# An encoder kernel on Trainium2: the first output weights split inside attention, the first output unit multiplied there

## The reference

```python
h = rms_norm(x, norm_mix_pre[l])
z = h @ w_in[l]                        # split into heads of three kinds
oa = mla_mixer(...)                    # 4 heads, latent attention, rotary key
ob = dilated_mixer(...)                # 4 heads, dilated windows and a relative bias
oc = gqa_axial_mixer(...)              # 8 query heads on 2 key heads
mix = concatenate([oa, ob, oc]) @ w_out[l]
x = x + rms_norm(mix, norm_mix_post[l])
h = rms_norm(x, norm_ffn_pre[l])
x = x + rms_norm(conv_gated_mlp(h, w_up[l], conv_w[l], conv_b[l], w_down[l]), norm_ffn_post[l])
```

## Time and profile before

| what | value |
|---|---|
| median of 3 runs | 3733.16 us (3732.81 to 3735.91) |
| the profiled execution's own time | 3736.56 us |
| its span in the profile | 3734.7 us |
| mean granted clock of TensorE | 0.988 |
| PE, DVE, ACT, POOL busy | 97%, 49%, 42%, 30% |
| attention of layer 0, layer 1 (barrier to barrier) | 324.7 to 806.3, 2169.4 to 2649.9 us |
| projection of layer 0, layer 1 | 806.3 to 965.6, 2649.9 to 2809.4 us |

### The profile page before, as it was taken

The page is one execution under the profiler, slowest core; times in us unless marked ns, Lnnn a source line. Parts: engine busy times, 40 slices in busy tenths (PEclk is TensorE's granted clock), DMA queues, the critical chain, the costliest instruction groups (busy, mean ns, idle before and its releaser), DMA issues. The chain is left out here.

```text
span 3734.7 us, 49829 instructions
## 1 busy us (share of the span) xinstructions
PE 3638.0 (97%) x18267; PEld 3008.3 (81%) x18267; DVE 1846.1 (49%) x2900; ACT 1564.6 (42%) x2527; POOL 1138.5 (30%) x827
## 2 busy tenths in 40 slices
PE   8999999989999999999999999999899999999998
PEld 7787777768788888888767877777788888888886
DVE  4135868954543333444551367699363333344335
ACT  4344878974311222221342367789552221221213
POOL 1233443433412221221342334433343221221213
PEclk9999999999999999999999999999999999999999
DMA  5442321023111111111324323110231111111113
GB/s 172 126 108 67 77 66 33 22 69 102 46 34 45 39 34 39 34 45 34 113 67 142 97 71 81 47 40 26 68 102 46 40 37 36 39 39 34 34 45 113
DMA packets 205964, 233.99 MB, mean 63 GB/s; under 512 B 15968, under 2 KB 164486, under 8 KB 205767
## 3 DMA queue, kind: packets, MB, share of 16 engines
q1 hardware_dynamic: 205807, 231.93, 21.1%
HBM read 173.86 MB, written 51.48 MB: 60 GB/s over the span
## 5 line engine op out<-in xcount | busy, mean ns | idle before, releaser
L222 PE MATMUL ps<-hh,wh 128*128 128x512 f32 (+1 forms) x2688 | 969.9, 361 | 15.4 <-PEq L216 11.5
L223 PE MATMUL ps<-hl,wh 128*128 128x512 f32 (+1 forms) x2688 | 955.9, 356 | 0.0
L224 PE MATMUL ps<-hh,wl 128*128 128x512 f32 (+1 forms) x2688 | 954.9, 355 | 0.0
L2466 POOL TENSOR_TENSOR wl<-raw,wh 128x1024 fp32r<-128x1024 f32 x126 | 301.7, 2401 | 1267.2 <-ACT wh L2299 1267.2
L222 PEld LDWEIGHTS ps<-hh,wh 128*128 128x128 f32 x2688 | 510.7, 190 | 93.8 <-issue 18.0
L2527 DVE SCALAR_TENSOR_TENSOR cb<-ps,params,cb 128x1023 f32<-128x1023 f32 (+1 forms) x172 | 143.9, 878 | 870.4 <-ACT cb L2308 870.4
L223 PEld LDWEIGHTS ps<-hl,wh 128*128 128x128 f32 x2688 | 511.0, 190 | 76.3 <-issue 5.7
L224 PEld LDWEIGHTS ps<-hh,wl 128*128 128x128 f32 x2688 | 510.1, 190 | 72.1
L1557 DVE TENSOR_TENSOR pl<-ps,ph 128x512 fp32r<-128x512 f32 (+1 forms) x576 | 375.0, 652 | 54.3 <-ACT ps L1402 53.9
L1511 DVE TENSOR_REDUCE mx<-ps 128x1 f32<-128x512 f32 x480 | 330.5, 689 | 141.8 <-PE ps L1316 82.9
L1401 ACT ACTIVATE ph<-ps 128x512 fp32r<-128x512 f32 (+1 forms) x576 | 329.6, 572 | 157.5 <-PE ps L1282 152.3
(11 more groups left out here) (265 smaller groups left out, 5644.8 us busy)
## 6 DMA issues: line engine op xcount, KB each, us to landing
raw<-in_w_up SPq DMA_DIRECT2D x88, 512.0 KB, 3.9
heads<-stage SPq DMA_DIRECT2D x38, 640.0 KB, 3.1
raw<-in_w_down SPq DMA_DIRECT2D x44, 512.0 KB, 3.7
rq<-heads SPq DMA_DIRECT2D x56, 320.0 KB, 4.8
raw<-in_w_in SPq DMA_DIRECT2D x32, 512.0 KB, 4.4
rk<-heads SPq DMA_DIRECT2D x32, 320.0 KB, 4.7
raw<-in_w_out SPq DMA_DIRECT2D x16, 512.0 KB, 4.3
residual<-my SPq DMA_DIRECT2D x32, 256.0 KB, 2.0
```

What stands on the lines that cost most here:

```text
L222: pe.matmul(out, wh, xh, start=(k == 0), stop=False)
L223: pe.matmul(out, wh, xl, start=False, stop=False)
L224: last = pe.matmul(out, wl, xh, start=False, stop=(k == len(pairs) - 1))
L2466: pool.tensor_tensor(c.wl[slot][:], c.raw[parity][:], c.wh[slot][:].bitcast(F32), ALU.subtract).then_inc(w_lo, units)
```

## The change

- **Attention.** SP now loads six units of w_out: 0 and 1 as before, 2 to 5 each when the unit two before it has its low part. It waits at the end for all six. GpSimd splits units 0 to 3 itself, high part by a copy and low part by a subtraction (`split_out_weights`), at steps 5 and 11 of heads 14 and 15, ahead of the output splits of these steps. After its last matmul of attention PE waits for the last two side results (bank 1 is theirs), the low part of unit 0 and the split output block 0 of head 15, and multiplies output unit 0 of block 0 into bank 1. A semaphore `early_unit` tells the next phase.
- **Projection.** PE starts with unit 1; whoever waited for `unit_done` waits for `early_unit` (unit 0) or one less. ScalarE starts with the evacuation of unit 0, splits units 4, 5, then 6 and 7; GpSimd makes the low parts of units 4 to 7. SP loads units 6 and 7. `early_unit` joins the list of semaphores cleared at the end of this phase.
- **Tiles.** Twelve weight tiles lie behind `my` and are dealt out so that the ones written in attention lie over memory that the last heads don't use; units 6 and 7 of w_out use wh0, wl0, wh1, wl1; units 0 and 1 of w_up the tiles of output units 0 and 1, unit 2 of w_up wh2, wl2.
- **Tables.** The table loads at the head of ScalarE's streams in attention and in projection are gone.

```diff
--- before.py
+++ after.py
@@ -164,6 +164,7 @@
     c.q2 = [take("q2_0", [P, T], F32R), q2_1, take("q2_2", [P, T], F32R)]
+    k1_0_at = at[0]
     c.k1 = [take("k1_0", [P, T], F32R), k1_1]
@@ -180,9 +181,10 @@
     c.my = [take(f"my{i}", [P, KC, 512]) for i in range(2)]
-    c.mw_hi, c.mw_lo = list(c.wh[0:2]), list(c.wl[0:2])
-    c.mw_hi += [take(f"mw_hi{n}", [P, KC, P], F32R) for n in range(2, KC)]
-    c.mw_lo += [take(f"mw_lo{n}", [P, KC, P], F32R) for n in range(2, KC)]
+    assert at[0] >= k1_0_at
+    tiles = [take(f"mw{n}", [P, KC, P], F32R) for n in range(12)]
+    c.mw_hi = [tiles[n] for n in (0, 2, 6, 8, 10, 4)] + c.wh[0:2]
+    c.mw_lo = [tiles[n] for n in (1, 11, 7, 9, 3, 5)] + c.wl[0:2]
     c.mx_ring = [take(f"mx_ring{i}", [P, 512]) for i in range(5)]
@@ -601,6 +603,7 @@
 NM = len(MAXES)
+OUT_EARLY = 4
 ROW_TILES = ((0, 4), (8, 10), (4, 8))
@@ -1190,7 +1193,7 @@
 
-        weights = sem("weights")
+        weights, out_w_hi, out_w_lo = [sem("weights0"), sem("weights1")], sem("out_w_hi"), sem("out_w_lo")
         scored, exp_done, p_low, pv_done = sem("scored"), sem("exp_done"), sem("p_low"), sem("pv_done")
@@ -1244,9 +1247,12 @@
                 sp.wait_ge(scored, NS * 14)
+                for n in range(OUT_EARLY + 2):
+                    if n >= 2:
+                        sp.wait_ge(out_w_lo, n - 1)
+                    sp.dma_start(c.raw[n % 2][:], out_unit(c, L, n)).then_inc(weights[n % 2], 16)
                 for i in range(2):
-                    sp.dma_start(c.raw[i][:], out_unit(c, L, i)).then_inc(weights, 16)
-                sp.wait_ge(weights, 32)
+                    sp.wait_ge(weights[i], 16 * (OUT_EARLY // 2 + 1))
 
@@ -1352,10 +1358,15 @@
 
+                for item in side_order[-2:]:
+                    pe.wait_ge(*side_read(item))
+                pe.wait_ge(out_w_lo, 1)
+                pe.wait_ge(out_lo, 3 * (HEADS - 1) + 1)
+                product(pe, bank(c, 1), [(c.mw_hi[0][:, k, :], c.mw_lo[0][:, k, :], c.hh[:, k, 0:512], c.hl[:, k, 0:512])
+                                         for k in range(KC)]).then_inc(c.early_unit, 1)
+
             @block.scalar
             def _(act):
-                act.preload_act_table_set(LOG_SET)
-
                 def split_k(h, b):
@@ -1481,6 +1492,14 @@
 
+                def split_out_weights(n):
+                    pool.wait_ge(weights[n % 2], 16 * (n // 2 + 1))
+                    settle((0, P), out_w_hi, n + 1)
+                    pool.tensor_copy(c.mw_hi[n][:], c.raw[n % 2][:]).then_inc(out_w_hi, 1)
+                    pool.wait_ge(out_w_hi, n + 1)
+                    settle((0, P), out_w_lo, n + 1)
+                    pool.tensor_tensor(c.mw_lo[n][:], c.raw[n % 2][:], c.mw_hi[n][:].bitcast(F32), ALU.subtract).then_inc(out_w_lo, 1)
+
                 for b in range(3):
@@ -1495,6 +1514,8 @@
                         lo_table(h + 1, i - 4)
+                    if i in (5, 11) and h in (HEADS - 2, HEADS - 1):
+                        split_out_weights(2 * (h - HEADS + 2) + i // 11)
                     for o in ended(g, PV_LAG + 3):
@@ -1560,7 +1581,7 @@
                        v_lo, max_scored, max_taken, max_ready, row_turned, row_copied, scored, exp_done, p_low, m_padded,
-                       pv_done, ln_done, rden_done, scaled, out_hi, out_lo, weights])
+                       pv_done, ln_done, rden_done, scaled, out_hi, out_lo, out_w_hi, out_w_lo] + weights)
 
@@ -1610,13 +1631,26 @@
 
-            return (c.mw_hi[n], c.mw_lo[n]) if n < KC else (c.wh[n - KC], c.wl[n - KC])
+            if n == KC + 2:
+                return c.wh[2], c.wl[2]
+            return c.mw_hi[n % KC], c.mw_lo[n % KC]
+
+        def split_count(n):
+
+            return n - OUT_EARLY + 1
+
+        def wait_unit(engine, x):
+
+            if x == 0:
+                engine.wait_ge(c.early_unit, 1)
+            else:
+                engine.wait_ge(unit_done, x)
 
...
                 def load_raw(n, src):
-                    sp.wait_ge(w_lo, n - 1)
+                    sp.wait_ge(w_lo, split_count(n - 2))
                     sp.dma_start(c.raw[n % 2][:], src).then_inc(raw_arrived[n % 2], 16)
@@ -1629,7 +1663,7 @@
 
-                for n in range(2, KC):
+                for n in range(OUT_EARLY + 2, KC):
                     load_raw(n, out_unit(c, L, n))
@@ -1653,7 +1687,7 @@
                 for i in range(2):
-                    sp.wait_ge(raw_arrived[i], 16 * 5)
+                    sp.wait_ge(raw_arrived[i], 16 * 3)
                 sp.wait_ge(stored, 16 * 3 * KC)
@@ -1669,8 +1703,8 @@
                     x = KC * b + n
-                    if b == 0:
-                        pe.wait_ge(w_lo, n + 1)
+                    if b == 0 and n >= OUT_EARLY:
+                        pe.wait_ge(w_lo, split_count(n))
                     if x >= 4:
@@ -1696,13 +1730,13 @@
                     if b == 0:
-                        pe.wait_ge(w_lo, KC + u + 1)
+                        pe.wait_ge(w_lo, split_count(KC + u))
                     products(o, KC + u, b, range(chunks))
...
 
-                for n in range(KC):
+                for n in range(1, KC):
                     out(n, 0)
@@ -1730,20 +1764,18 @@
             def _(act):
-                act.preload_act_table_set(LOG_SET)
-
                 def split(n):
-                    if n >= 2:
-                        act.wait_ge(raw_arrived[n % 2], 16 * (n // 2))
+                    if n >= OUT_EARLY + 2:
+                        act.wait_ge(raw_arrived[n % 2], 16 * ((n - OUT_EARLY) // 2))
                     if n >= KC:
-                        act.wait_ge(unit_done, 2 * KC + n - KC + 1 if n < KC + 2 else 3 * KC)
+                        wait_unit(act, 2 * KC + n - KC if n < KC + 2 else 3 * KC - 1)
                     act.activation(weight(n)[0][:], c.raw[n % 2][:], ACT.Copy).then_inc(w_hi, 1)
...
                     src = bank(c, OUT_BANKS[x % 4], w)
-                    act.wait_ge(unit_done, x + 1)
+                    wait_unit(act, x)
                     if b == 1 and n >= 5:
@@ -1800,13 +1832,10 @@
 
-                for n in range(3):
-                    split(n)
                 take(0, 0)
-                split(3)
                 split(4)
+                split(5)
                 take(1, 0)
-                split(5)
                 split(6)
@@ -1862,7 +1891,7 @@
                     wh, wl = weight(n)
-                    pool.wait_ge(w_hi, n + 1)
+                    pool.wait_ge(w_hi, split_count(n))
                     pool.tensor_tensor(wl[:], c.raw[n % 2][:], wh[:].bitcast(F32), ALU.subtract).then_inc(w_lo, 1)
@@ -1880,7 +1909,7 @@
 
-                for n in range(KC):
+                for n in range(OUT_EARLY, KC):
                     low_weight(n)
@@ -1973,7 +2002,7 @@
                                              in1=c.cb[0][:, t0:t0 + s - 1], op0=ALU.mult, op1=ALU.add).then_inc(shifted, 1)
-        end_phase(nc, raw_arrived + [w_hi, w_lo, unit_done, evacuated, squared, acc_added, summed, logged, root] + x_in +
+        end_phase(nc, raw_arrived + [c.early_unit, w_hi, w_lo, unit_done, evacuated, squared, acc_added, summed, logged, root] + x_in +
                   [scaled, added_pool, added_dve, stored, new_squared, new_added, new_summed, new_logged, new_root,
@@ -2709,6 +2738,7 @@
 
+    c.early_unit = nc.alloc_semaphore("early_unit")
     c.latents_stored = nc.alloc_semaphore("latents_stored")
...
     c.q_raw = nc.alloc_semaphore("q_raw")
```

## The result

The changed kernel took 3712.36 us in the median of five runs (3707.99 to 3718.05) against 3732.81 in the median of five of before (3730.74 to 3735.91): ratio 0.9946, 95% interval 0.9935 to 0.9957, so 16 to 24 us faster. The forecast was 3712.3. The profiled execution took 3715.99 us, span 3714.2.

A forecast was written before the change was run, and what follows sets the result against it. TensorE, busy 97%, bounds the kernel; only the hole at the attention-projection seam can be won. 22.2 - 1.06 + 0.2 = 21.3, less 0.2 a layer, 20.9 us; 3733.16 - 20.9 = 3712.3 us, range 3709.5 to 3717.5.

The forecast's parts named there:

- The seam: Between attention and output projection: early unit fills PE's hole, unit 1 starts 11.2 us (layer 0) and 11.0 us earlier.
- The clock after the gap: PE's gaps of 1.33 and 1.50 us before unit 1: no slow restart; bound 1.7 us a layer.
- the 1.86 row: Profile row at 1828.59: after 1.86 us idle, PE's granted clock was 0.66 over the next 5 us.
- The longer clear: Barrier at projection's end: early_unit widens the cleared semaphore range, 1.06 us lost over both layers.
- GpSimd's splits: Attention's heads 14 and 15: four splits, cast about 1.2 plus subtraction 2.34 us each, cost nothing.
- the cover that the step named: Output block 0 of head 15 is done at 798.66, 2.1 us before PE's early product needs it.
- VectorE: Attention's heads 14 and 15: GpSimd's splits beside VectorE don't block it, subtractions at most 693 ns, no cost.
- Table loads: Loads ahead of attention and projection go: projection's counted in the seam, attention's 0.2 us in layer 1, bounds 0 and 1.28.
- The sum: Whole kernel: 22.2 - 1.06 + 0.2 = 21.3, less 0.2 a layer, 20.9 us gained, giving 3712.3.
- The 0.4 taken off for the restart and semaphore steps: Both seams: an estimated 0.2 us a layer for the first matmul after a wait and a few semaphore steps.
- the forecast's own span: Kernel time from 3710.3 (short clear, whole table load, no 0.4) to 3713.5 us, within the forecast's 68%.
- rival 1: PE restarts slowly after attention's barrier: 3.4 us lost over both layers, 3715.7; one layer 3714; chance 22%.

The follow-up runs named there:

- the kernel that takes it back: Changed kernel with two early semaphores, one per layer, cleared only at the very end instead of at projection's end: 3714.75 us, ratio to before 0.9946.
- the three sets of the changed kernel: The changed kernel, unchanged, measured on three occasions: medians 3712.36, 3715.42 and 3714.38 us, ratios to before 0.9946, 0.9949 and 0.9944.

## Why the prediction was right

By its steps:

- *The seam.* 11.2 and 11.0 us forecast, 11.15 and 11.01 measured; gaps 1.33 and 1.50 forecast, 1.36 and 1.53 measured, of which 0.02 each is attention's own clear (673 and 844 ns, from 652 and 825), whose growth the step had put at nothing. That PE and not GpSimd ends the barrier shows at 804.91 against 803.50.
- *The clock after the gap.* Kept, as the step said. Its reason, that both gaps lie under 1.74, which kept its clock, has held in all 58 gaps up to that length. Of the 1.86 row it took too much: a gap of that length lost the clock in 18 cases of 24, and 1.97 and 2.29 kept it, so above 1.74 the rows give no edge but a risk.
- *The longer clear.* 1.06 forecast, 0.649 + 0.430 = 1.08 measured, and shown to count one for one by the kernel that takes it back.
- *GpSimd's splits.* 1.2 for the cast, 1.04 measured; 2.34 for the subtraction, 2.40. Free, with the cover that the step named, and free even if packed into one head: attentions whose first 40 us had the same clock (0.96) took 473.2 to 473.4 us with the splits and 473.23 without.
- *VectorE.* Not touched, 693 ns at most. On the shared port the Trainium skill (SBUF — State Buffer, section SBUF: two separate sides) names only VectorE operations with two SBUF inputs, or in a mode with two ports; here the VectorE operation has one input in PSUM, and the trace agrees.
- *Table loads.* Projection's was worth its 1.28 us of hole in each layer, but only 0.6 of seam in the runs compared. For attention's in layer 1 the step took 0.2. In the changed kernel the first Exp starts at 2159.01, 0.97 behind PE's first matmul at 2158.04; in the kernel before it was 0.99. So 0.02: that term was ten times too large, and too small to matter. Where ScalarE does change its function set, ahead of Gelu, the switch took the load alone: in the trace of before the copy ahead ends at 967.96, the load runs from 967.97 and Gelu starts at 969.27.
- *The sum.* 22.2 - 1.06 less 0.2 is about 20.9, and the traces' own account of these terms is 22.16 - 1.08 = 21.1. The 0.4 taken off for the restart and semaphore steps came to 0.1 in the two seams (7.23 and 7.40 us where the steps give 7.16 and 7.33). The lower end of the forecast's own span is 3710.6 by its terms (3733.16 - 22.2 + 0.89 - 1.28), not 3710.3, and its terms don't give the upper end, 3713.5; neither bears on the result. The ratios of the three sets of the changed kernel (0.9946, 0.9949, 0.9944) times 3733 make 19 to 21 us.

The range, 8 us wide, was made of rival 1 and of 3 us of spread. The medians kept to it, but five of the sixteen single runs did not (3706.79 to 3721.80), since the spread was taken from three runs of before that lay close together. The mechanism behind it, a clock kept or lost behind PE's idle stretches, stood in the prediction only for the new gap; that layer 0's attention gained 2.17 us by it in the profiled run and layer 1's lost 1.65 is chance that nearly cancels.

## What to carry to other kernels

Between two phases, look for the engine that bounds both and ask which of its next work needs nothing of the last results: a product moved into the wait hides its own time, and if what is left of the gap is short, it spares the restart at the lower clock, here about 2 us a time. What stands behind a barrier to feed that engine can be done ahead of it by an engine with slack. And when PE waits only for the barrier, the barrier's own parts are the next thing: a clear of semaphores costs by the range of numbers it spans, and not by how many of them the phase uses, so keep a phase's semaphores side by side.

## What the runs showed of the hardware

- A clear took 129 ns for 17 semaphore numbers, 198 for 31, 285 for 48, 411 for 69, 847 for 150 (the ranges counted from the programs' numbers), so 5 to 6 ns for each further one, and PE waited for all of it, starting 0.19 us behind its end. The 17 and the 48 belong to the same list of 17 semaphores, in layer 0 and in layer 1.
- After PE stood still for 1.80, 2.12, 2.65 or 2.82 us the granted clock of the next 5 us was 0.66 to 0.69; after 1.97 and 2.29 it was 1.00. After 1.86 or 1.87 us it was 0.66 in 18 cases and 1.00 in 6; after 1.36 to 1.74 it was 1.00 in all 58.
- The same attention of the same kernel took 473.3 or 475.9 us, with a granted clock of 0.96 or 0.87 over its first 40 us behind a gap of 3.0 to 3.2 us. Why it is one or the other was not tried.
- In the one profile with the shorter hole (8.90 and 9.06 us, not 10.18 and 10.34) the lower clock held for 14 and 13 matmuls, not 11 and 10, so half of what the missing table load gave was lost again. That the shorter hole is the cause is not shown: behind 5.41 and 5.58 us it was 9 and 13.
